# Expert outputs of a mixture of experts: a scratch in memory and an indirect gather, or one-hot products on TensorE

## The reference

```
# x + hierarchical_moe(rmsnorm(x)) in each layer; T = 512 tokens, 32 experts
g_sel   = argmax(x @ w_group + b_group)                 # 1 of 4 groups
top_i   = top 2 of the 8 experts of that group          # 2 experts per token
weights = softmax share of the group * share of the expert among the two
for each expert e, for each token that chose it:
    hid = silu(x @ w1[e]) * (x @ w3[e])                 # 1024 -> 512
    y   = hid @ w2[e]                                   # 512 -> 1024
    out[token] += weight * y
```

## Time and profile before

| | |
|---|---|
| time, median of 3 runs | 1718.62 us (1717.81 to 1719.45) |
| profiled execution, its own time | 1712.28 us |
| its span, first to last instruction | 1710.5 us, granted TensorE clock 0.946 |
| TensorE busy | 1487.4 us (87%) |
| VectorE busy | 589.2 us (34%) |
| ScalarE busy | 342.2 us (20%) |
| mean over the span from memory | 285 GB/s |

### The profile page before, as it was taken

How to read it: one execution, slowest core, us unless ns; L and a number is a source line. 1 busy time by engine, 2 the same in 40 slices (tenths; PEclk the granted TensorE clock), 3 DMA queues, 4 the chain that set the end, 5 groups by cost and what they waited for, 6 DMA issues and landing times.

```text
span 1710.5 us, 39733 instructions
## 1 busy us (share of the span) xinstructions
PE 1487.4 (87%) x16237; PEld 1003.0 (59%) x16238; DVE 589.2 (34%) x1383; ACT 342.2 (20%) x669; POOL 37.6 (2%) x68
## 2 busy tenths in 40 slices
PE   8999999898888989864999989989998999866663
PEld 7888888655554655532787844457555556533332
DVE  5347632322222222213634356733222222211113
ACT  5441313200000000001432344524100000000000
POOL 3000000000000000001000000000000000000001
PEclk9999999999999999977999999999999999988887
DMA  5621226799999999999212122055899997999995
GB/s 202 223 98 54 95 98 243 289 419 421 425 422 422 421 425 414 422 421 344 79 54 99 50 95 78 25 197 227 351 423 421 422 409 313 412 422 423 420 422 188
DMA packets 100998, 487.04 MB, mean 285 GB/s; under 512 B 10736, under 2 KB 22896, under 8 KB 84304
## 3 DMA queue, kind: packets, MB, share of 16 engines
q1 hardware_dynamic: 76544, 457.19, 65.5%
q10 hardware_dynamic: 20528, 17.10, 3.1%
q0 software_dynamic: 3872, 11.98, 2.2%
HBM read 467.58 MB, written 18.64 MB: 284 GB/s over the span
## 4 chain that ended last, share of the span: by engine, by line
issue 52%; DMA 21%; PE 21%; ACTq 3%; DVE 2%; POOL 1%; ACT 0%; SPq 0%; POOLq 0%; DVEq 0%
DMA y_rows<-SCR 13%; DMA EB<-in_m_w 7%; PE ps L1174 5%; PE ps L1176 5%; PE ps L1175 5%; ACTq L623 3%; PE ps L1304 1%; PE ps L1384 1%; DMA EB<-y_rows,pos_i 1%; PE ps L1319 1%; PE ps L1170 1%; DVE X L939 1%; PE ps L1286 1%; POOL EB L484 1%; DMA gain<-in_a_norm 0%
## 5 line engine op out<-in xcount | busy, mean ns | idle before, releaser
L1304 PE MATMUL ps<-EB,SCR 128*32 128x256 f32 x6016 | 379.2, 408 | 106.9 <-DMA EB<-in_m_w 81.2
L1304 PEld LDWEIGHTS ps<-EB,SCR 128*32 128x32 f32 x6016 | 219.2, 118 | 259.3 <-issue 171.4
L896 DVE TENSOR_TENSOR SCR<-SCR,ps 64x256 f32<-64x256 f32 x94 | 39.7, 423 | 615.3 <-ACT SCR L611 615.3
L1176 PE MATMUL ps<-EB_r 128*128 128x512 f32 x512 | 201.0, 393 | 0.0
L1319 PE MATMUL ps<-EB,SCR 128*32 128x256 f32 x3008 | 186.1, 388 | 1.9 <-issue 0.3
L1286 PE MATMUL ps<-H,SCR 128*32 128x256 f32 x3072 | 185.7, 380 | 0.0
L616 ACT ACTIVATE SCR<-ps 128x256 f32 (+1 forms) x94 | 36.0, 383 | 601.8 <-issue 439.8
L1286 PEld LDWEIGHTS ps<-H,SCR 128*32 128x32 f32 x3072 | 108.0, 111 | 58.8 <-issue 1.5
L1319 PEld LDWEIGHTS ps<-EB,SCR 128*32 128x32 f32 x3008 | 106.7, 111 | 55.8 <-issue 21.9
L1174 PE MATMUL ps<-EB_r,H_r 128*128 128x512 f32 x320 | 128.0, 400 | 1.0 <-DVE EB L972 1.0
L1175 PE MATMUL ps<-EB_r,H_r 128*128 128x512 f32 x320 | 126.1, 394 | 0.0
(11 more groups left out here) (218 smaller groups left out, 1391.4 us busy)
## 6 DMA issues: line engine op xcount, KB each, us to landing
EB<-in_m_w SPq DMA_DIRECT2D x192, 2048.0 KB, 10.1
EB<-in_a_w_in SPq DMA_DIRECT2D x8, 2048.0 KB, 9.2
y_rows<-SCR ACTq DMA_DIRECT2D x376, 32.0 KB, 5.9
EB<-in_a_w_out SPq DMA_DIRECT2D x4, 2048.0 KB, 7.8
EB<-in_kv_w SPq DMA_DIRECT2D x4, 2048.0 KB, 14.9
EB<-in_b_w_qg SPq DMA_DIRECT2D x4, 2048.0 KB, 8.2
y_rows<-X SPq DMA_DIRECT2D x2, 2048.0 KB, 15.7
SCR<-ncum_rows ACTq DMA_DIRECT2D x16, 256.0 KB, 3.5
```

The costliest lines, as they stand in the source:

```text
L896: v.tensor_tensor(hid[0:HALF, :], silu[HALF:P, :], ps[0][HALF:P, 0:CW], ALU.mult).then_inc(m["hid"], 1)
L1176: return mm(o, left[1], right[0], start=False, stop=stop)
L1304: last = mm(ps[0][g * CAP:(g + 1) * CAP, 0:CW], xT[:, k, :], w[:, k, g % 2 * CW:(g % 2 + 1) * CW], start=k == 0, stop=k == KD - 1)
```

## The change: what it does

The scratch, its stores, its fill and the indirect gathers go. Instead:

- A table `slot_w` gives each row of an item its routing weight, made once per layer by POOL's one-hots (`item_tables`) and 32 small products on TensorE.
- ScalarE copies the down product times that weight to fp32r (`y_hi`), and VectorE puts the rest, product minus high part, beside it (`y_lo`), both in `y_parts`, two items side by side.
- VectorE makes for each item a one-hot over 256 tokens on the partitions of the item's slots (`spread_tokens`), from a row of positions per token, for both items of a pair.
- TensorE's `move` multiplies them: for a pair of items and half of the tokens, 32 products (2 token tiles, 2 items, high and low part, 4 column blocks), each with 32 rows, 128 columns of one-hot and 256 moving columns. The four column blocks lie on four row tiles and write to four PSUM banks. One half of the tokens is done in each iteration, so each pair is moved in two iterations.
- VectorE adds the result to two token tiles of X in each iteration.

After the loop two more moves and four adds finish the stream. The copy and split of the next projection's rows is in another order on ScalarE and VectorE, and keep_busy has other counts. The down product now goes to the right half of ps2.

```diff
-        ysb = scr(7 * CW, 9 * CW)
+        slot_w = scr(6 * CW, 6 * CW + MAX_ITEMS)
...
+        spread, spread_end = (SCR_r[:, a:a + 2 * CW].rearrange("p (i n) -> p i n", i=2) for a in (SP0, SP0 + 2 * CW))
+        y_parts = SCR_r[:, Y0:Y0 + 4 * CW].rearrange("p (i k n) -> p i k n", i=2, k=2)
+        pos_row = scr(POS0, POS0 + 2 * T).rearrange("p (k n) -> p k n", k=2)
...
-        ps = [ctx.enter_context(nc.psum_tensor(f"ps{i}", [P, COL], F32)) for i in range(8)]
+        ps_four = [ctx.enter_context(nc.psum_tensor(f"ps{i}", [P, 4 * COL], F32)) for i in range(2)]
+        ps = [ps_four[i // 4][:, i % 4 * COL:(i % 4 + 1) * COL] for i in range(8)]
+        moved = [b[:, :].rearrange("p (g t n) -> p g t n", g=CG, t=2) for b in ps_four]
...
-                r = SLOTS + (i - 2) * T
-                if r < Y_ROWS:
-                    sp.dma_start(y_rows[r:r + T, :].rearrange("(p t) n -> p t n", t=NT), X[:, :, :])\
-                        .then_inc(y_filled, 16)
...
-            def gather_outputs(l):
+            def item_tables(l):
                 m = moe[l]
-                pool.wait_ge(m["y_complete"], 1)
-                for t in range(NT):
-                    for k in range(2):
-                        g.indirect_dma_start(
-                            out=y_got[:, 2 * t + k, :], out_offset=None, in_=y_rows[:, :],
-                            in_offset=bass.IndirectOffsetOnAxis(ap=pos_i[:, 4 * k + t:4 * k + t + 1], axis=0),
-                        ).then_inc(m["y_got"][t], 16)
+                pool.wait_ge(lists_in, 2 * l + 1)
+                for i in range(2):
+                    g.memset(spread[:, i, :].bitcast(F32), 0.0).then_inc(m["spread"], 1)
+                for k in range(2):
+                    g.memset(y_parts[:, :, k, :].bitcast(F32), 0.0).then_inc(m["y_lo" if k else "y_hi"], 1)
+                pool.wait_ge(pos_split, 3 * l + 3)
+                for i in range(2 * NT):
+                    g.tensor_scalar(slot_hot[:, i, :], iota_c[:, :], pos_slot[:, i:i + 1], None, ALU.is_equal).then_inc(hot, 1)
+                pool.wait_ge(w12_ready, 2 * l + 2)
+                for i in range(2 * NT):
+                    g.tensor_scalar(item_hot[:, i, :], item_slot[:, 2:2 + MAX_ITEMS], pos_item[:, i:i + 1],
+                                    w12[:, i:i + 1], ALU.is_equal, ALU.mult).then_inc(hot, 1)
...
                 total = act.value_load(n0_i[0:1, NE:NE + 1], min_val=1, max_val=MAX_ITEMS)
...
-                def item_silu(n):
+                act.wait_ge(slot_w_done, 2 * l + 1)
+                a.activation(slot_w, ps[6][:, 0:MAX_ITEMS], ACT.Copy).then_inc(slot_w_done, 1)
+                act.wait_ge(slot_w_done, 2 * l + 2)
+                with act.Fori(0, total) as n:
                     act.wait_ge(m["up"], n + 1)
                     a.activation(silu[HALF:P, :], ps[0][0:HALF, 0:CW], ACT.Silu).then_inc(m["silu"], 1)
-                def item_output(n):
                     act.wait_ge(m["down"], n + 1)
-                    a.activation(ysb[:, bass.ds((n & 1) * CW, CW)], ps[4][:, 0:CW], ACT.Copy).then_inc(m["y_out"], 1)
-                def store_before(n):
-                    act.wait_ge(m["y_stored"], 16 * CG * n + 1)
-                    act.wait_ge(m["y_out"], n + 1)
-                    for g in range(CG):
-                        act.dma_start(y_rows[bass.ds(n * CAP - CAP, CAP), g * CW:(g + 1) * CW],
-                                      ysb[g * CAP:(g + 1) * CAP, bass.ds(((n + 1) & 1) * CW, CW)])\
-                            .then_inc(m["y_stored"], 16)
-                act.wait_ge(y_filled, 16 * ((Y_ROWS - SLOTS) // T))
-                item_silu(0)
-                item_output(0)
-                with act.Fori(1, total) as n:
-                    item_silu(n)
-                    store_before(n)
-                    item_output(n)
-                store_before(total)
-                if before_end is not None:
-                    before_end()
-                act.wait_ge(m["y_stored"], 16 * CG * total + 16 * CG + 1)
...
+                    a.activation(y_parts[:, bass.ds(n & 1, 1), 0, :], ps[2][:, CW:2 * CW].unsqueeze(1), ACT.Copy,
+                                 scale=slot_w[:, bass.ds(n, 1)]).then_inc(m["y_hi"], 1)
...
+                def spread_tokens(dst, which, items, link, ready):
+                    toks = [pos_row[:, k, bass.ds(which * 2 * P, 2 * P)] for k in range(2)]
+                    for i in range(2):
+                        link(v.tensor_scalar(dst[:, i, :], toks[0], item_slot[:, bass.ds(items[i] + 2, 1)], None,
+                                             ALU.is_equal), i)
+                    for i in range(2):
+                        v.scalar_tensor_tensor(dst[:, i, :], toks[1], item_slot[:, bass.ds(items[i] + 2, 1)],
+                                               dst[:, i, :].bitcast(F32), ALU.is_equal, ALU.add).then_inc(ready, 1)
...
+                dve.wait_ge(slot_w_done, 2 * l + 1)
+                for k in range(2):
+                    dve.wait_ge(row_done, 2 * l + k + 1)
+                    then(v.tensor_scalar(pos_row[:, k, :], ps[(4, 7)[k]][:, :], slot_p[:, :], None, ALU.subtract))
+                spread_tokens(spread_end, 0, (total - 2 + (total & 1), total - 1 + (total & 1)), lambda ins, i: then(ins),
+                              end_spread)
+                dve.wait_ge(slot_w_done, 2 * l + 2)
+                v.memset(cn[:, 0:1], 0.0).then_inc(m["added"], 1)
...
                     item_xT(n + 1)
+                    dve.wait_ge(m["moved"], n + 1)
+                    for t in range(2):
+                        X_t = X[:, bass.ds((n & 1) * 2 + t, 1), :].rearrange("p a (g n) -> p (a g) n", g=CG)
+                        add = v.tensor_tensor(X_t, X_t, moved[1][:, :, t, :], ALU.add)
+                    add.then_inc(m["added"], 1)
                     def link(ins, k):
                         ins.then_inc(m["step"], 1)
-                        dve.wait_ge(m["step"], 2 * n + k + 1)
-                    select(n + 2, m, 0, link)
+                        if k >= 2:
+                            dve.wait_ge(m["step"], 4 * n + k)
+                    spread_tokens(spread, (n + 1) & 1, (n - 1 + ((n + 1) & 1), n - 1 + (n & 1)),
+                                  lambda ins, i: link(ins, i + 1), m["spread"])
+                    select(n + 2, m, 0, lambda ins, k: link(ins, k + 2))
+                    dve.wait_ge(m["y_hi"], n + 2)
+                    v.scalar_tensor_tensor(y_parts[:, bass.ds(n & 1, 1), 1, :], ps[2][:, CW:2 * CW].unsqueeze(1),
+                                           slot_w[:, bass.ds(n, 1)], y_parts[:, bass.ds(n & 1, 1), 0, :].bitcast(F32),
+                                           ALU.mult, ALU.subtract).then_inc(m["y_lo"], 1)
+                spread_tokens(spread, 1, (total - (total & 1), total - 2 + ((total + 1) & 1)), lambda ins, i: then(ins),
+                              end_spread)
+            def add_moved(l, t):
+                m = moe[l]
+                dve.wait_ge(end_moved, 2 * l + t // 2 + 1)
+                X_t = X[:, t, :].rearrange("p (g n) -> p g n", g=CG)
+                v.tensor_tensor(X_t, X_t, moved[1 - t // 2][:, :, t % 2, :], ALU.add).then_inc(x_moe, 1)
...
-            split_tile(T_K)
-            combine(0, 0)
-            scaled_rows("kv", hrow, combine=lambda t: combine(0, t + 1) if t + 1 < NT else None,
-                        after=lambda t: rows_lo("kv", t))
-            rows_lo("kv", NT - 1)
+            for t in range(2):
+                add_moved(0, t)
+            dve.wait_ge(x_moe, 2)
+            scaled_rows("kv", hrow, blocks=(0,))
+            for t in range(2, NT):
+                add_moved(0, t)
+            dve.wait_ge(x_moe, NT)
+            scaled_rows("kv", hrow, blocks=(1,))
+            split_tile(T_K, 0, 2)
+            rows_lo("kv", 0)
+            split_tile(T_K, 2, 4)
+            rows_lo("kv", 1)
+            for t in range(2, NT):
+                scaled_rows("kv", hrow, blocks=(t,))
+                rows_lo("kv", t)
...
+                def move(banks, sides):
+                    for t in range(2):
+                        for i in range(2):
+                            for k in range(2):
+                                for g in range(CG):
+                                    rows = slice(g * CAP, (g + 1) * CAP)
+                                    last = mm(moved[banks][:, g, t, :], sides[rows, i, t * P:(t + 1) * P],
+                                              y_parts[rows, i, k, :], start=i == 0 and k == 0, stop=i == 1 and k == 1)
+                    return last
+                def move_items(n):
+                    pe.wait_ge(m["spread"], 2 * n + 2)
+                    pe.wait_ge(m["y_hi"], n + 1)
+                    pe.wait_ge(m["y_lo"], n + 1)
+                    pe.wait_ge(m["added"], n + 1)
+                    move(1, spread).then_inc(m["moved"], 1)
...
+                        move_items(n)
                         gather(n + 1)
...
```

(46 more changed lines are left out.)

148 lines of the change are left out of this document (85 added, 63 removed).

## The result

The changed kernel takes **1765.4 us** (median of 4 runs, 1765.0 to 1767.9) against 1718.2 for the kernel before (4 runs, 1716.2 to 1719.5): a ratio of 1.0275, 95% interval [1.0261, 1.0289]. That is +47 where +24.7 was forecast. All times are in us, L numbers in this part are lines of the changed kernel.

What follows compares the result with a forecast made beforehand. Weight loads at 420 GB/s were taken to bound the kernel. Layer 0 +23.7, layer 1 +24.7 and the ends -11.8 and -11.9 sum to +24.7 on 1718.6: 1743 us, range 1711 to 1785.

Steps and rivals of the forecast that it cites:

- The bound moves from weights to the item: Heavy part of each layer: items at 9.8 us set the pace, DMA share falls to 0.89 and 0.81.
- The move, 1.15: TensorE, per item: 8 waves of 0.115 us, one load ahead and a change of tiling, 1.15 in all.
- each wave pays its weight load: Rival for TensorE's move: 8 x 0.11 = 0.9 us more, period 10.7, +85, 1804 us; chance 0.11.
- row tiles take turns: Rival for TensorE's move: products one after another, 3.7 us, period 12.3, +190 us; chance 0.04.
- the rule that was weighed: TensorE's move: a weight load overlaps products only on a different row group, 0.9 us more; kept as a rival, 0.11.
- The loop, 9.8: Heavy items: gather, VectorE's work to y_lo at +8.55, semaphores 0.1 and the move 1.15 make a period of 9.8 us.
- Two semaphore steps 0.1: Between the end of VectorE's y_lo and the start of TensorE's move in each item: 0.1 us.
- TensorE alone, 9.2: Rival: TensorE's own 8.06 + 1.15 sets the item period, 9.2 us, 0.7 per expert switch; +4, 1723; chance 0.08.
- The prelude, +0.5 a layer: Ahead of each layer's first up: position products, small products and POOL's one-hots make it 0.5 us later (0 to 3).
- Weights' step, 14.9: Experts with one item each: 14.9 us per expert instead of 15.13, since the stores are gone.
- the buffers' rule: Single items at a layer's end can't catch up, because three buffers bound how far the loads are ahead.
- The ends: Last up to the projection in layer 0, -11.8 us; last up to the end in layer 1, -11.9 us.

Runs made afterwards that it cites:

- The reordering: The changed kernel with y_lo computed on VectorE ahead of the next selection instead of behind it: 1745.3 us, ratio 1.0183 to the kernel before.
- the exact version that came out level: The changed kernel with y_lo ahead of the selection, item one-hots on VectorE and one expert register reused on TensorE: 1719.7 us, ratio 1.001 to the kernel before.

## Why the prediction was right, and where its sizes were off

The direction and the mechanism held; the time forecast was 22 short, in spans 31. Of these 31 the heavy items' loop has 14.6, the first items 4.3, the single items 2.2, the preludes 6.1 and the ends 3.8. Two ends of ranges were off by a little: at 67 per us the periods 9.3 and 10.4 give 1710 and 1783.5, not 1711 and 1785.

- *The bound moves from weights to the item.* Right: DMA share 0.94 then 0.83 in layer 0's heavy part and 0.82 in layer 1's (forecast 0.89 and 0.81), SP's wait for up 146 (forecast 80 or more), y_lo what the move waits for, VectorE without a gap. The reordering showed it by itself: -20. One reading was too broad: "DMA share 1.01 at 420 GB/s in both mixtures" holds for layer 0 and for layer 1's single items, but layer 1's heavy part stood at 0.95 and was near the items' pace before the change. The sum doesn't use it.
- *The move, 1.15.* Measured 1.15. Neither "each wave pays its weight load" nor "row tiles take turns" happened. The single records settle the rule that was weighed: from the third wave on, a wave's four weight loads (0.18 each) each start within 0.01 of a product of the wave before, which lies on the same row tile, and the waves still follow each other by 0.12. The Trainium skill (TensorE: Matmul & The Clock Gate, Part 3, "The mechanism") has a load overlap running products only where the row group differs. This trace disagrees: each load here runs beside a product of its own row tile, as the spacing reads. It agrees with the same section's other sentence, by which a load may also go ahead into a background weight buffer.
- *The loop, 9.8: mis-sized.* It was 10.02 in layer 0 and 10.13 in layer 1. y_lo ended at +8.61 (forecast 8.55). "Two semaphore steps 0.1" is the wrong term: from y_lo's end to the move's first product 0.25 to 0.29 pass. The 0.11 more in layer 1 is a wait of 0.27 instead of 0.16 between the comparisons and the comparison-and-adds; in the run with the one-hots on VectorE it was gone (10.02), with that part of the loop unchanged. Its cause stays open. 0.22 for 38 items and 0.33 for 27 make 8.4 + 8.9 = 17.3, less 2.7 for switches that cost less than the 0.2 each had: 14.6 of the 21.1 by which the two stretches from first to last up were short.
- *The first item of each layer* took 11.96 instead of 9.8, +2.2 each. It was priced like any other. Up ran at half clock there (1.7 more), and the switch to the second expert, 0.9, stood in the open. In the run with the one-hots on VectorE up had full clock (3.66), and the move waited 0.8 instead for VectorE's position rows and the one-hots for the end, which stand ahead of the first gate product: 11.49 in layer 0, 11.05 in layer 1. So when one cause is gone the other shows.
- *TensorE alone, 9.2.* It is 9.34: the step from up to the move is 3.59, not the 3.47 of up to gather in the earlier trace rows. With y_lo first this became the bound.
- *The prelude, +0.5 a layer: mis-sized.* +2.0 and +5.1, for GpSimd's sixteen instructions, which had no price of their own in that 0.5, took 7.4 in one chain. In layer 0 the gather, with less filler ahead of it, started 2.3 earlier than before (321.75 against 324.03), which made up for half. VectorE's took it back: -9.7.
- *Weights' step, 14.9.* Measured 14.91, and the buffers' rule (nothing is caught up at the end) held: from item 39 to the last up 91.7 (forecast 90.1), from item 28 in layer 1 219.7 (219.1).
- *The ends.* -12.5 and +3.1 behind it against -14.1 and +2.3; -10.5 against -11.9. In layer 0 tile 0's low part was ready at 846.1, 28.0 after the last up as forecast; what came last were 24 filler products ahead of the projection, at half clock:

```profile
844.46 3.61 PE L1213 MATMUL ps<-tri_in,tri 128*128 128x128 f32 x24
847.83 0.47 PE L1217 MATMUL ps<-EB_r,H_r 128*128 128x512 f32 x1
```

  (PEclk 0.69 from 843 to 848). In layer 1 the 1.4 is mostly the last up's own wait for y_lo, 0.8, which the steps left out.

## What to carry to other kernels

A transfer-bound kernel has slack on its engines, and that slack is a number per item. Here an item of layer 0's heavy part, with its share of the switches, took 9.10 before (346.0 for 38), of which TensorE alone needs about 8.5 (8.06 and some 18 of switches). The saved time at the ends and in the single items buys a little more: the exact version that came out level took 9.57 (363.5). Before work is moved onto an engine to save bytes, add up the loop that it closes (each engine's instructions, 0.25 for a semaphore between engines, the switches of the loop around it) and compare with that number; past it, the saved bytes buy nothing. When such a loop is too long, first put the instruction that another engine waits for ahead of those that nobody waits for: it cost nothing and gave 20 us.

## What the runs showed of the hardware

- Row tiles of 32 rows run side by side even where the program gives each tile its products in a row: 32 fp32r products of 256 columns took 1.27 with four of a tile in a row, 1.15 in turn.
- With ScalarE's copy that scales by a column of numbers and writes fp32r (L633) a table load of 1.28 stands in front of every SiLU, 94 in all, where the kernel before, whose copy (L616) did neither, had one per layer. What brings it is not shown: the copy of the router's rows (L616 of the changed kernel), which scales by a column too, comes between square roots without a new table load (8 copies, one load a layer). In the loop over items it starts as soon as the copy is done and lies under up, so it delays nothing:

```profile
504.24 0.48 ACT L633 ACTIVATE SCR_r<-ps,SCR 128x256 f32 x1 [6.48 <-PE ps L1381]
504.73 1.28 ACT L630 ACT_TABLE_LOAD   x1
508.12 0.38 ACT L630 ACTIVATE SCR<-ps 64x256 f32<-64x256 f32 x1 [2.10 <-PE ps L1366]
```

- Eight two-step comparisons of 128x64 in a row take GpSimd 4.69, 0.59 each, and VectorE 1.88, 0.235 each; eight of one step and 128x32 take GpSimd 2.69, 0.34 each.
- TensorE's switch between experts is its two register loads of 0.30, each with some 0.45 of address and check steps around it. They run while the last down products are still under way, and what is left over is the 0.67: with one load and its steps less it became 0.03.
